# A two-layer sparse-attention decoder step on one Trainium2 core: selection rounds, weight loads and weight splitting put in another order

## The reference

```python
def indexer_scores(qi, wi, ki):
    dots = jnp.einsum('bqhd,bsd->bqhs', qi, ki) * (D_IDX ** -0.5)
    return jnp.einsum('bqh,bqhs->bqs', wi * (N_IDX_HEADS ** -0.5), jax.nn.relu(dots))

# prompt rows, in blocks of 128 queries
sc = jnp.where(key_pos <= q_pos, indexer_scores(qi, wi, ki), -jnp.inf)
_, idx = lax.top_k(sc, top_k)                # keys chosen for each query
o = gathered_attention(q, k[idx], v[idx], valid=idx <= q_pos)

# one layer, h = rms_norm(x)
q, k, v, ga, qi, wi, ki, ub, gb, cv, cg, gc = split_columns(h @ w_in)
q, k = partial_rope(rms_norm(q)), partial_rope(rms_norm(k))     # 16 of 64 dims are rotated
conv = silu(layer_norm(depthwise_conv31(cv * sigmoid(cg))))
pool = (trailing means of width 2, 4, 8, 16 minus the token) @ w_pool * scale
x = x + concat([att * silu(ga), pool * silu(gb), conv * silu(gc)]) @ w_out
```

## Time and profile before

| | |
|---|---|
| median of 3 runs | 736.61 us (736.46 to 740.76) |
| profiled execution | 738.43 us, span 737.1 us |
| mean granted TensorE clock | 0.974 |
| PE busy | 688.2 us (93%), 5314 matmuls |
| DVE busy | 521.5 us (71%), 1312 instructions |
| ACT busy | 342.5 us (46%) |
| POOL busy | 311.1 us (42%) |
| chain that ended last, by engine | PE 43%, DVE 21%, POOL 14%, ACT 10%, DMA 5% |

### The profile page before, as it was taken

One profiled execution on the slowest core, in us unless ns is written; L12 is line 12 of the kernel. 1 busy time (PEld: TensorE's weight loads), 2 busy tenths in 40 slices (PEclk: granted clock), 3 DMA queues, 4 the chain that ended last, 5 costly groups with the idle time before them and its releaser, 6 DMA issues.

```text
span 737.1 us, 14658 instructions
## 1 busy us (share of the span) xinstructions
PE 688.2 (93%) x5314; PEld 576.1 (78%) x5314; DVE 521.5 (71%) x1312; ACT 342.5 (46%) x884; POOL 311.1 (42%) x463
## 2 busy tenths in 40 slices
PE   5999989799889989999999998978989898999998
PEld 5987868588787777768999686757878787777797
DVE  4358989899977876445733998999997795722232
ACT  5747536245946433333245762734484643332202
POOL 1403599963947600111250259997384861000000
PEclk9999999899989999999999999999998998999999
DMA  5460240314223525015016213131423164401302
GB/s 206 141 196 19 69 135 30 116 36 145 59 89 112 201 70 199 0 58 174 22 59 190 58 60 101 75 116 36 145 59 89 58 174 145 172 1 58 103 20 109
DMA packets 54984, 71.97 MB, mean 98 GB/s; under 512 B 12977, under 2 KB 30585, under 8 KB 54881
## 3 DMA queue, kind: packets, MB, share of 16 engines
q1 hardware_dynamic: 54802, 70.96, 30.0%
q10 hardware_dynamic: 111, 0.08, 0.0%
HBM read 64.05 MB, written 7.61 MB: 97 GB/s over the span
## 4 chain that ended last, share of the span: by engine, by line
PE 43%; DVE 21%; POOL 14%; ACT 10%; DMA 5%; issue 4%; SPq 2%; DVEq 0%; POOLq 0%; ACTq 0%
PE R L1347 16%; DVE bias L1791 5%; DVE small L1789 4%; PE R L1331 4%; PE R L1332 3%; PE R L1333 3%; POOL small L907 3%; ACT W_r L986 3%; ACT W L986 3%; PE R L1490 3%; DVE W_r L1695 3%; POOL kz L911 3%; PE A L1519 2%; PE A L1277 2%; POOL kz L909 2%
## 5 line engine op out<-in xcount | busy, mean ns | idle before, releaser
L1331 PE MATMUL R<-x_hi,W_r 128*128 128x268 f32 x448 | 138.6, 309 | 5.9 <-DVE cc L1695 1.8
L865 POOL TENSOR_TENSOR W_r<-W,W_r 128x256 fp32r<-128x256 f32 x128 | 92.1, 751 | 114.7 <-ACT W_r L986 114.0
L1333 PE MATMUL R<-x_hi,W_r 128*128 128x268 f32 x448 | 132.4, 295 | 0.0
L1332 PE MATMUL R<-x_lo,W_r 128*128 128x268 f32 x448 | 132.2, 295 | 0.0
L1347 PE MATMUL R<-yT,W 128*128 128x268 f32 (+2 forms) x768 | 124.2, 318 | 0.0
L1347 PEld LDWEIGHTS R<-yT,W 128*128 128x128 f32 x768 | 106.9, 190 | 15.8 <-issue 7.1
L1306 PE MATMUL R<-W_r,x_hi 128*128 128x512 f32 (+2 forms) x252 | 98.8, 392 | 15.1 <-DVE W_r L1695 11.5
L1331 PEld LDWEIGHTS R<-x_hi,W_r 128*128 128x128 f32 x448 | 88.6, 198 | 22.0 <-issue 10.6
L1307 PE MATMUL R<-W_r,x_hi 128*128 128x512 f32 (+2 forms) x252 | 95.6, 379 | 0.0
L1308 PE MATMUL R<-W_r,x_lo 128*128 128x512 f32 (+2 forms) x252 | 95.2, 378 | 0.0
L1332 PEld LDWEIGHTS R<-x_lo,W_r 128*128 128x128 f32 x448 | 88.9, 198 | 0.0
(11 more groups left out here) (277 smaller groups left out, 1300.4 us busy)
## 6 DMA issues: line engine op xcount, KB each, us to landing
W<-in_w_in SPq DMA_DIRECT2D x52, 512.0 KB, 4.8
KV<-in_cache_k SPq DMA_DIRECT2D x32, 256.0 KB, 2.9
W<-in_w_out SPq DMA_DIRECT2D x8, 1024.0 KB, 7.5
KV<-in_cache_v SPq DMA_DIRECT2D x32, 256.0 KB, 3.4
ubx<-qkv_rows SPq DMA_DIRECT2D x16, 256.0 KB, 3.4
out_new_k_prompt<-kz SPq DMA_DIRECT2D x8, 256.0 KB, 2.0
out_new_v_prompt<-V SPq DMA_DIRECT2D x8, 256.0 KB
out_y_prompt<-W SPq DMA_DIRECT2D x8, 256.0 KB
```

What stands on the lines that cost most here:

```text
L865: done = pool.tensor_tensor(w_raw(m, W_r)[part], w_raw(m)[part], w_high(m, W_r)[part].bitcast(F32), ALU.subtract)
L1331: pe.matmul(out, hi[:, cols], x_hi[:, kc, toks], start=(kc == 0), stop=False)
L1332: pe.matmul(out, hi[:, cols], x_lo[:, kc, toks], start=False, stop=False)
L1333: m = pe.matmul(out, lo[:, cols], x_hi[:, kc, toks], start=False, stop=(kc == KC - 1))
```

## The change

- `REST_ON_POOL`: the rests of slots 8 to 12 are GpSimd's, all made ahead of its first tile; those of 13, 16 and 17 go to VectorE, behind taps of tiles 1, 6 and 7. The rests of 14, 15 (18, 19) are put between the first taps of tile 4 (9), where they stood behind all its taps. GpSimd makes rests 24 and 25 ahead of the pooling sums.
- `HIGH_AT` and the places of `high` in `scalar_layer` follow that. `QUADS_IN` puts each quad one place earlier.
- `TURN_BEHIND` puts the turn and keep of q tiles 7 to 9 behind v units, one later than q tile 6; the others stay three behind.
- SP loads slots 14 to 17 behind the store of k tile 0 (before: of tile 1) and slots 18 to 21 ahead of the store of the q row.
- The rotation makes its two half-width products as one of full width.
- Selects: `EARLY_TO` is 35, 12 and 0 for tiles 2, 3, 4 (before: 32, 28, 6); `between` makes three more in the conv units; in steps 0 to 3 there are none, and from step 4 on three per step that has any, tile 3 first, then tile 4 up to step 28 (before: two of tile 4 per step up to step 19, with tiles 2 and 3 in steps 0 to 3).

```diff
@@ -82,7 +82,7 @@
 NTH = [1 + sum(1 for x in range(AHEAD, m) if slot(x) == slot(m)) for m in range(len(LOADS))]
-REST_ON_POOL = [FIRST[G["k"]] + 2, FIRST[G["k"]] + 3, FIRST[G["q"]], FIRST[G["q"]] + 1, FIRST[G["v"]], FIRST[G["v"]] + 1] + list(range(FIRST[G["ub"]], FIRST[-1]))
+REST_ON_POOL = list(range(FIRST[G["k"]], FIRST[G["q"]] + 1)) + list(range(FIRST[G["ub"]], FIRST[-1]))
@@ -158,18 +158,19 @@
 GATE_OF = {u: g for g, (u, _) in enumerate(GATES)}
-QUADS_IN = {("conv", 1, 0): {7: 0}, ("conv", 0, 1): {3: 1, 7: 2}, ("conv", 1, 1): {4: 3}, ("conv", 2, 0): {1: 4, 6: 5},
-            ("conv", 2, 1): {3: 6}, ("conv", 3, 0): {1: 7, 6: 8}, ("conv", 3, 1): {3: 9}}
+QUADS_IN = {("conv", 1, 0): {3: 0, 7: 1}, ("conv", 0, 1): {3: 2, 7: 3}, ("conv", 1, 1): {4: 4}, ("conv", 2, 0): {1: 5, 6: 6},
+            ("conv", 2, 1): {3: 7}, ("conv", 3, 0): {1: 8, 6: 9}}
+TURN_BEHIND = {3: 0, 4: 1, 5: 2, 6: 3, 7: 4, 8: 5, 9: 6, 11: 7, 12: 8, 13: 9}
 assert len(PIECES) == 40
...
 PAIRED = sum(1 for i, _ in ITEMS if WIDTH[i] <= 512)
-HIGH_AT = {1: 22, 2: 23, 3: 24, 4: 25, 7: 26, 8: 27, 13: 28, 14: 29}
+HIGH_AT = {0: 22, 1: 23, 2: 24, 3: 25, 7: 26, 8: 27, 13: 28, 14: 29}
 TAPS_K, TAPS_Q = (3, 3, 3, 3, 3), (3, 3, 3, 3, 4)
 NO_ROUND = (9, 10, 12, 16, 18)
-EARLY_TO, EARLY_REST = {1: 2 * LOW_ROUNDS + 3, 2: 32, 3: 28, 4: 6}, 5
+EARLY_TO, LATE_FROM = {1: 2 * LOW_ROUNDS + 3, 2: 2 * ROUNDS + 1, 3: 12}, 4
 CONV_END, PD_END, LN_END = 2 * CONV_W + 12, 14, 7
@@ -741,17 +742,16 @@
                     row_k.did(sp.dma_start(qkv_dram[1], kz[0:8, n % KZ, :]))
-            for n in range(2):
-                k_store(n)
+            k_store(0)
             for m in range(14, 18):
                 w_load(m)
-            for n in range(2, NT):
+            for n in range(1, NT):
                 k_store(n)
+            for m in range(18, 22):
+                w_load(m)
             n = NT + KQ_ORDER.index(0)
...
             row_q.did(sp.dma_start(qkv_dram[0], kz[0:8, n % KZ, :]))
-            for m in range(18, 22):
-                w_load(m)
             def v_store(i):
@@ -880,8 +880,9 @@
                 s.did(pool.tensor_tensor(ta, z[:, :, 0:2 * half], cos.broadcast_to([r, heads, 2 * half]), ALU.mult))
-                s.did(pool.tensor_tensor(tb[:, :, 0:half], z[:, :, half:2 * half], sin[:, :, 0:half].broadcast_to([r, heads, half]), ALU.mult))
-                s.did(pool.tensor_tensor(tb[:, :, half:2 * half], z[:, :, 0:half], sin[:, :, half:2 * half].broadcast_to([r, heads, half]), ALU.mult))
+                swapped = z[:, :, 0:2 * half].rearrange("p h (two x) -> p h two x", two=2)[:, :, ::-1, :]
+                s.did(pool.tensor_tensor(tb.rearrange("p h (two x) -> p h two x", two=2), swapped,
+                                         sin.rearrange("p h (two x) -> p h two x", two=2).broadcast_to([r, heads, 2, half]), ALU.mult))
                 pool.wait_ge(*s.at(s.n))
@@ -914,18 +915,15 @@
                 pool.wait_ge(*kz_s.at(n + 1))
-            rest(10)
-            rest(11)
-            rest(12)
+            for m in range(8, 13):
+                rest(m)
             pool.wait_ge(*gam_s.at(32))
...
                 kq_tile(n)
-                if n == 0:
-                    rest(13)
-                if n in (5, 6):
-                    rest(11 + n)
             for m in range(20, 24):
+                rest(m)
+            for m in (24, 25):
                 rest(m)
@@ -944,9 +942,6 @@
             pool.wait_ge(*ps_s.at(4))
-
-            for m in (24, 25):
-                rest(m)
             wait_evac(pool, ("lnsum", 0, 0))
@@ -1095,13 +1090,11 @@
                     relu(p)
-                if n in (0, 1):
-                    high(6 + n)
-                if n in (4, 5):
+                if n in (0, 2):
+                    high(6 + n // 2)
+                if n in (4, 5, 6, 7):
                     high(4 + n)
-                if n in (6, 7):
-                    high(4 + n)
-                if n == 7:
+                if n == 8:
                     half_tanh(0)
@@ -1112,18 +1105,16 @@
                     high(13)
-                if n >= 3:
-                    kq_keep(n - 3)
+                if n in TURN_BEHIND:
+                    kq_keep(TURN_BEHIND[n])
             for n in range(NT, 2 * NT):
-                if n in (5, 6):
-                    scale_block(11 + n)
+                if n in (6, 7):
+                    high(10 + n)
                 if n == 9:
...
                 kq_evac(n)
-                if n in (5, 6):
-                    high_block(11 + n)
-                kq_keep(n - 3)
+                kq_keep(TURN_BEHIND[n])
             for n, i in enumerate(KQ_ORDER):
@@ -1133,8 +1124,8 @@
                     evA.did(copy(V[0:ROWS_P[i], i, :], R[0:ROWS_P[i], bank(("v", i, 0)), :], rinv[0:ROWS_P[i], i:i + 1]))
-                if n < 3:
-                    kq_keep(7 + n)
+                if 2 * NT + n in TURN_BEHIND:
+                    kq_keep(TURN_BEHIND[2 * NT + n])
                 if n in (2, 3):
@@ -1451,8 +1442,8 @@
                     unit_tm((name, i, 0), name)
-                if 3 <= n < 2 * NT + 3:
-                    kq_turn(n - 3)
+                if n in TURN_BEHIND:
+                    kq_turn(TURN_BEHIND[n])
                 if n == 2 * NT + 2:
@@ -1762,6 +1753,10 @@
                 last[i, lo] = acc_s.n
+            def gather_four(quad):
+                for p in range(4 * quad, 4 * quad + 4):
+                    gather(p)
+
             steps_of, mark, slot_of = {1: 0, 2: 0, 3: 0, 4: 0}, {}, {1: 3, 2: 0, 3: 1, 4: 2}
@@ -1794,15 +1789,9 @@
             def late(n):
-                if n < EARLY_REST:
-                    select(2)
-                    select(3)
-                if n not in NO_ROUND:
-                    select(4)
-                    if n < EARLY_REST:
-                        select(2)
-                        select(3)
-                    select(4)
+                if n >= LATE_FROM and n not in NO_ROUND:
+                    for _ in range(3):
+                        select(3 if steps_of[3] <= 2 * ROUNDS else 4)
             def tap(j):
@@ -1823,35 +1812,37 @@
                 _, m, h = u
-                if u == ("conv", 1, 1):
-                    rest(7)
-                for quad in QUADS_IN.get(u, {}).values():
-                    for p in range(4 * quad, 4 * quad + 4):
-                        gather(p)
+                quads = QUADS_IN.get(u, {})
+                for kc in quads:
+                    if kc < KC - 1:
+                        gather_four(quads[kc])
                 wait_unit(dve, u)
...
                     evD.did(dve.tensor_tensor(bufB[:, m - 2, tok(h)], src, row[:, tok(h)], ALU.mult))
+                if u == ("conv", 1, 0):
+                    rest(6)
                 if u == ("conv", 0, 1):
-                    rest(6)
-                if u == ("conv", 2, 1):
-                    rest(8)
-                if u == ("conv", 3, 0):
-                    rest(9)
+                    rest(7)
+                if KC - 1 in quads:
+                    gather_four(quads[KC - 1])
                 if m >= 2:
-                    between(1)
+                    between(1 if u == ("conv", 2, 0) else 2)
             conv_in(0)
...
             for n in range(2 * NT):
-                for _ in range((TAPS_K + TAPS_Q)[n]):
+                for x in range((TAPS_K + TAPS_Q)[n]):
                     tap(j)
                     j += 1
-                if n % NT == NT - 1:
-                    rest(14 if n < NT else 18)
-                    rest(15 if n < NT else 19)
+                    if n % NT == NT - 1 and x < 2:
+                        rest((14 if n < NT else 18) + x)
+                if n == 1:
+                    rest(13)
+                if n in (6, 7):
+                    rest(10 + n)
                 kq_sum(n)
@@ -1880,7 +1871,7 @@
                 for i in EARLY_TO:
-                    if steps_of[i] < EARLY_TO[i] and (i < 4 or steps_of[2] == EARLY_TO[2]):
+                    if steps_of[i] < EARLY_TO[i]:
                         select(i)
```

## The result

The changed kernel takes 757.3 us (median of 4 runs, 755.84 to 760.65) against 737.03 us: ratio 1.0272, 95% interval 1.0231 to 1.0313. It is slower, inside the forecast range (738 to 758) and 9 us above the forecast of 748.2. The profiled execution took 757.63 us, span 756.3, mean granted clock 0.955 (before 0.974).

What follows compares the result with a forecast made beforehand. No engine bounds all: TensorE from step 28, VectorE in steps 0 to 3, both by turns between. Layer sums +7.7 and +3.9 us on the profiled 738.4 gave 750.0, median 1.8 lower: 748.2 us, range 738 to 758.

Steps and rivals of the forecast that it cites:

- The deciding term, steps 18 to 27: Steps 18 to 27: 27 more selects on VectorE exceed its idle time, +15.1 us in layer 0, +10.8 in layer 1.
- Steps 4 to 17: Attention steps 4 to 17: 30 selects for 20, part in VectorE's idle time, +1.1 us layer 0, -0.4 layer 1.
- The front's time at step 0: Everything before step 0: TensorE reaches step 0 6.9 us sooner in layer 0, 4.6 in layer 1.
- VectorE's own part: VectorE's sum up to the last rest of v: 3.6 us sooner in layer 0, 2.7 in layer 1.
- Its waits for rounded parts: Before step 0: VectorE's waits for rounded parts of slots go, 3.9 us less in layer 0, 3.0 in layer 1.
- with that wait shorter I count the 1.6 us back, 1.0 of the slow matmuls behind it, and the 0.7 wait: Layer 0, TensorE from the second v unit: 1.6 us lost to low clock, 1.0 and 0.7 come back.
- Gain at step 4: At step 4, front's gain plus selects leaving earlier stages: 8.9 us sooner in layer 0, 6.9 in layer 1.
- The rotation: GpSimd's tiles before step 0: one product less saves 0.1 to 0.2 us a tile, nothing on the path.
- The clock rival: Steps 19 to 27: TensorE's clock falls behind waits, +4.9 us each layer, 758 us; chance 0.10.
- The front gains more: Cheaper rests before step 0 and less idle time in steps 4 to 27: 737 us, half of it 742.5; chance 0.13.
- given back after step 28: After step 28 VectorE's slack absorbs its lag, so 15.1 and 10.8 us vanish: 722 us; chance 0.05.

Runs made afterwards that it cites:

- front_old_sp_order: The changed kernel with the selects and SP's load order of the kernel before: 739.2 us, ratio 1.001.
- none_in_18_27: The changed kernel without the 27 selects of width 532 in steps 19 to 27 of each layer (output not the reference's): 729.8 us, ratio 0.9892.
- late_from_0: The changed kernel with three selects a step from step 0 on, so 12 fewer a layer in steps 18 to 27: 748.6 us, ratio 1.0156.
- rotation_only: The kernel before with only the rotation in one product less: ratio 0.9946 without its four highest executions; with all, medians 737.08 against 738.77 us.
- front_only: The changed kernel with all selects where the kernel before has them: 740.4 us, ratio 1.0033.

## Why the prediction was right, and where not

- **The deciding term, steps 18 to 27, was right.** Forecast +15.1 and +10.8 us, measured +16.5 and +10.7, with VectorE 50.65 us busy in layer 0, 49.66 in layer 1, and TensorE's waits released by VectorE. The length was taken as 52.0 of work and 2.5 of idle time; the profile has 50.65 busy and 5.35 idle. Some 2.2 of these 5.35 are, by my estimate, the 0.08 us from each of 27 selects to the next, which the forecast counts as work. In layer 0 the term is partly right by luck: the selects cost 13.0 us there, and the other 3.5 are the distance between two kernels without selects in this stretch, of which TensorE's slower matmuls (38.76 us busy for 36.35) may be 2.4.
- **Steps 4 to 17**: +1.1 and -0.4 forecast, +1.8 and +1.4 measured. This term came out near by luck: VectorE kept 7.0 us of idle time in layer 0, not the 3.5 that I took (my bound of 6 was passed), and it was busy 36.5 us, not the 39.4 that I counted. The two misses nearly cancel.
- **The front's time at step 0**: 6.9 us forecast in layer 0, 4.4 measured; 4.6 and 4.2 in layer 1. VectorE's own part was sized nearly right (3.6 forecast in layer 0, the rests of v end 4.4 us sooner, at 140.1 for 144.5; 2.7 forecast and 2.1 measured in layer 1; rests cost 0.991 us mean, 0.995 taken). Its waits for rounded parts did go, but `front_old_sp_order` shows that they go under SP's old order as well, which the forecast had not seen. The step that failed is "with that wait shorter I count the 1.6 us back, 1.0 of the slow matmuls behind it, and the 0.7 wait": the wait was not shorter, it was 4.10 us, since TensorE comes sooner as well and VectorE still ends last, and the v unit ran at 0.50. How fast TensorE goes behind that wait then differed between executions. `none_in_18_27` and `late_from_0` have the same instructions ahead of step 0: there TensorE needed 29.56 us from the end of the wait to step 0 at a mean clock of 0.94, in the changed kernel 32.05 at 0.86, and it was at step 0 at 164.84 and 165.07. So some 2.5 us of the miss in layer 0 are the clock's, and in those two executions the 6.9 us would have been passed.
- **Gain at step 4**: 8.9 and 6.9 forecast, 5.9 and 6.1 measured, for that reason.
- **The rotation** was costed at 0.1 to 0.2 us a tile "and nothing on the path". The size was right (1.4 us by the last of ten tiles in layer 0). Whether it is on the path is not shown: `rotation_only` lies 0.2 to 0.5% under before, by which of its executions are counted.
- **The clock rival** came true in its mechanism and not in its price: 0.85 and 0.87 in steps 18 to 27, TensorE busy 6.3 us more in layer 0 and 1.2 more in layer 1 by step starts, beside a VectorE that was busy for 50 us of each stretch. How much of the price of the selects is the clock's was not separated. The time it named, 758, is near the one measured by other terms.
- **"The front gains more" and "given back after step 28"** did not come: steps 28 to 39 take 61.95 us as before, and the lag of step 28 stays to the end of the layer.
- **What I had not seen** is that the front's gain and the selects' leaving are one thing. I summed them; `front_only` shows that the first is 0 without the second. The sum came out right because both were there.
- The median lies another 1.5 us higher than the profiled times say, of 9.1 us missed. Three sums of the prediction are off by little: its terms add up to 8.8 and 6.8 us at step 4 (8.9 and 6.9 there), and half the rival of a better front is 742.8, not 742.5.

## What to carry to other kernels

When one engine is full over several stages, work that leaves one of them frees time only if it lands where the engine has some; count its busy time from the first full stage to the place where it is next free, not by stage. A change that lets another engine come sooner is worth nothing until the full engine comes sooner as well, so test the parts alone and together. And a small move in time can cost elsewhere (here 2.7 to 4.4 us a layer) if it puts a two-operand VectorE instruction beside a row of GpSimd instructions: look for single instructions that last ten times their usual time before explaining a slow version by its edit, and look at the same place in the version that you compare with.

## What the runs showed of the hardware

- A VectorE instruction that needed 0.17 us lasted 6.02 us and ended with the last of eight GpSimd instructions issued back to back (200.59 to 206.1); it was not let in between them. It showed in three kernels, in both layers of each, with 6.00 to 6.03 us every time. In the other eleven kernels an evacuation of 0.44 us that comes later was held to the end of the same eight, for 1.38 to 4.14 us.
- The same v unit behind the same kind of wait took TensorE 6.33 us at a granted clock of 0.50 in the changed kernel; the whole stretch from the wait to step 0 took 32.05 us there at a mean clock of 0.86, and 29.56 at 0.94 in two kernels with the same instructions in it.
- The new rotation's one product with its halves swapped takes GpSimd 0.513 us mean for 128 columns in `rotation_only`, against two of 0.378 for 64. In the changed kernel the same product takes 0.626 and the one ahead of it 0.592 (0.500 before), so that a part of the gain goes again. VectorE has more two-operand work beside it there; that this is the reason was not tested. Its groups:

```profile
L884 POOL TENSOR_TENSOR rot_tmp<-kz,cst 128x128 f32<-128x128 f32 x16 | 10.0, 626 | 0.0
L882 POOL TENSOR_TENSOR rot_tmp<-kz,cst 128x128 f32<-128x128 f32 x16 | 9.5, 592 | 1.3
```
